# Table v of a PEER layer with 312 of 320 token columns on TensorE, the last eight tokens from gathered rows

## What is computed

```python
def block(args):
    xb, ib, gb = args                       # tokens, their 128 expert numbers, their 128 gates
    a = jax.nn.gelu(jnp.einsum('ted,td->te', u[ib], xb), approximate=False)
    return jnp.einsum('te,ted->td', gb * a, v[ib])
```

## Time and profile before

| what | us |
|---|---|
| median of 3 runs (4019.13 to 4028.27) | 4021.95 |
| the profiled execution | 4022.95 |
| its span, first to last instruction | 4021.3 |
| table v's matmuls, first to last start | 3082.2 to 3990.9 |

### The profile page before, as it was taken

The page is one execution under the profiler, slowest core; times in us unless marked ns, Lnnn a source line. Parts: engine busy times, 40 slices in busy tenths (PEclk is TensorE's granted clock), DMA queues, the critical chain, the costliest instruction groups (busy, mean ns, idle before and its releaser), DMA issues. The chain is left out here.

```text
span 4021.3 us, 70026 instructions
## 1 busy us (share of the span) xinstructions
PE 3856.3 (96%) x26200; PEld 3680.9 (92%) x26200; DVE 3056.9 (76%) x4100; ACT 1422.0 (35%) x2062; POOL 1496.8 (37%) x1285
## 2 busy tenths in 40 slices
PE   7999999999999887999999999999998999999997
PEld 7999988999999665999899999999998999999997
DVE  6875167777777433878679999999986888888887
ACT  5884122222223222223333333333333333333332
POOL 0000022323233122234215556655756555555551
PEclk9999999999999999999999999999999999999999
DMA  7988888999999797889679989888998999999996
GB/s 270 346 308 299 292 292 325 355 370 375 364 366 374 295 374 266 299 318 354 254 268 328 331 327 325 320 305 298 351 361 299 355 346 344 345 346 340 347 344 255
DMA packets 333939, 1310.11 MB, mean 326 GB/s; under 512 B 46800, under 2 KB 103280, under 8 KB 264192
## 3 DMA queue, kind: packets, MB, share of 16 engines
q1 hardware_dynamic: 201616, 646.09, 43.6%
q0 software_dynamic: 106800, 629.71, 42.5%
q10 hardware_dynamic: 25344, 31.99, 2.2%
HBM read 1237.86 MB, written 69.77 MB: 325 GB/s over the span
## 5 line engine op out<-in xcount | busy, mean ns | idle before, releaser
L130 PE MATMUL acc<-x_hi,w_hi 128*128 128x448 f32 x1296 | 478.0, 369 | 9.7 <-DVE w_lo L119 5.2
L130 PE MATMUL acc<-x_lo,w_hi 128*128 128x448 f32 x1296 | 476.3, 368 | 0.0
L114 ACT ACTIVATE w_hi<-w_raw 128x1024 fp32r<-128x1024 f32 x242 | 256.2, 1060 | 621.8 <-DMA w_raw<-in_w_gate 268.3
L130 PE MATMUL acc<-x_hi,w_lo 128*128 128x448 f32 x1296 | 476.1, 367 | 0.0
L2376 POOL DMA_INDIRECT routes_scratch<-gate_sums,route x320 | 389.0, 1216 | 139.0 <-issue 82.9
L119 DVE TENSOR_TENSOR w_lo<-w_raw,w_hi 128x1024 fp32r<-128x1024 f32 x242 | 295.6, 1223 | 185.7 <-ACT w_hi L114 184.7
L2793 POOL TENSOR_TENSOR tile_full<-act_and_gate 128x320 f32<-128x320 f32 x120 | 312.7, 2606 | 266.3 <-DVE tile_lo L2897 165.9
L2172 PE MATMUL acc<-h_hi,w_hi_b 128*128 128x320 f32 (+1 forms) x1152 | 367.4, 319 | 17.1 <-DVE w_lo_b L2162 16.9
L2154 ACT ACTIVATE w_hi_a<-w_raw 128x1024 fp32r<-128x1024 f32 x270 | 278.6, 1057 | 296.7 <-PE acc L2965 250.3
L2172 PE MATMUL acc<-h_hi,w_hi_a 128*128 128x320 f32 (+1 forms) x1152 | 367.8, 319 | 10.3 <-DVE w_lo_a L2162 9.4
L2154 ACT ACTIVATE w_hi_b<-w_raw 128x1024 fp32r<-128x1024 f32 x272 | 278.7, 1055 | 248.7 <-PE acc L2965 210.2
(11 more groups left out here) (525 smaller groups left out, 10244.5 us busy)
## 6 DMA issues: line engine op xcount, KB each, us to landing
w_raw<-in_w_peer_u SPq DMA_DIRECT2D x256, 512.0 KB, 6.5
w_raw<-in_w_peer_v SPq DMA_DIRECT2D x256, 512.0 KB, 5.8
w_first<-in_w_gate SPq DMA_DIRECT2D x96, 512.0 KB, 4.9
w_raw<-in_w_gate SPq DMA_DIRECT2D x96, 512.0 KB, 7.3
w_first<-in_w_z SPq DMA_DIRECT2D x66, 512.0 KB, 5.0
w_raw<-in_w_z SPq DMA_DIRECT2D x66, 512.0 KB, 7.2
k_ring<-in_cache_k SPq DMA_DIRECT2D x64, 512.0 KB, 6.8
v_ring<-in_cache_v POOLq DMA_DIRECT2D x64, 512.0 KB, 8.0
```

Source lines behind the costliest of these rows:

```text
L114: nc.scalar.activation(w_hi[:, j % 4, :], raw[:, j % 4, :], ACT.Copy).then_inc(q["hi"], 1)
L130: last = nc.tensor.matmul(dst, l_, r_[:, cc, 0:cn], start=(cc == first and p_ == 0), stop=(cc == last_c and p_ == 2))
```

## The change

The last eight of the 320 tokens are left out of table v's dense product, which then has NV = 312 columns. (`act_and_gate`, the tiles and `out_t` have 312 columns too.) For these eight tokens the 8 x 128 rows of v that they use are gathered: eight gathers of 128 rows, where partition p of gather k holds an expert of token p // 16. DVE multiplies each row by its weight and adds it to `sum8` (128 x 2048), in four quarters of 512 columns. At the end four matmuls with a matrix of zeros and ones (`pick`) add the 16 partitions of each token and put the sums into rows 56 to 63 of block 3, which DVE adds to x.

What this puts where:

- SP, after the load of x1's block 0: stores expert numbers, routes and gates of the eight tokens to DRAM, waits for that, and loads them in the other layout.
- POOL, after the rows of pass 1: eight gathers of single numbers (the activations), a wait for them, the weights `w8`, and the first gather of rows (`last_gather(0)`). One more `last_gather` stands ahead of the tiles of each of the stretches 1 to 7, behind a wait for the last quarter of the row before. `row8` is a single buffer.
- DVE: one quarter behind the second step of each pass of the second part of stretches 0 to 6, and of the first part of stretch 7.
- PE: the four matmuls ahead of the third pass of the last part.

```diff
-        t_hi = at("tile_hi", [P, 2 * GRP, ND], F32R, O_R1)
+        t_hi = at("tile_hi", [P, 2 * GRP, NV], F32R, O_R1)
...
+        row8 = at("rows_of_last_tokens", [P, D], F32, O_R1 + 4 * GRP * ND * 4 + 2 * D * 4)
+        sum8 = at("sum_of_last_tokens", [P, D], F32, O_R1 + 4 * GRP * ND * 4 + 3 * D * 4)
...
             sp.dma_start(x1[:, 0, :], x1_dram[COLS[0]:COLS[0] + P, :]).then_inc(s_xback, 16)
+            last8 = slice(ROWS[3] - VTOK, ROWS[3])
+            for k, x_ in enumerate((eidx, route, gate.bitcast(I32))):
+                sp.dma_start(last8_dram[k], x_[last8, 3, :]).then_inc(s_8st, 16)
+            sp.wait_ge(s_8st, 48)
+            for k, x_ in enumerate((e8, r8, g8.bitcast(I32))):
+                sp.dma_start(x_[:], last8_dram[k].rearrange("t (j k) -> (t j) k", k=VTOK)).then_inc(s_8ld, 16)
             with sp.Fori(1, (NTILE - GRP) // 2) as i:
...
+            def last_gather(k):
+                nc.gpsimd.tensor_copy(stage_8[:, 0:1], e8[:, k:k + 1] if isinstance(k, int) else e8[:, bass.ds(k, 1)]).then_inc(s_8sg, 1)
+                pool.wait_ge(s_8sg, k + 1)
+                pool.sem_inc(s_8tick, 1)
+                pool.indirect_dma_start(row8[:], None, a["peer_v"], bass.IndirectOffsetOnAxis(ap=stage_8[:, 0:1], axis=0)).then_inc(s_8gat, 16)
+
...
             for s in range(2):
                 product(s + GRP, s, 1)
-            with pool.Fori(1, (NTILE - GRP) // 2) as i:
+            rows(1, True)
+            pool.wait_ge(s_8ld, 48)
+            for k in range(VTOK):
+                pool.indirect_dma_start(a8[:, k:k + 1], None, acts_dram.rearrange("n p (t o) -> (n p t) o", o=1), bass.IndirectOffsetOnAxis(ap=r8[:, k:k + 1], axis=0)).then_inc(s_8a, 16)
+            pool.wait_ge(s_8a, 16 * VTOK)
+            nc.gpsimd.tensor_tensor(w8[:], a8[:], g8[:], ALU.mult).then_inc(s_8w, 1)
+            last_gather(0)
+            with pool.Fori(2, GRP) as i:
+                rows(i, True)
+            with pool.Fori(1, NG // 2 - 1) as gg:
+                pool.wait_ge(s_8used, 4 * gg + 1)
+                last_gather(gg)
+                with pool.Fori(0, GRP) as j:
+                    rows(GRP * gg + j, True)
+            pool.wait_ge(s_8used, 4 * (VTOK - 1) + 1)
+            last_gather(VTOK - 1)
+            with pool.Fori(GRP * (NG // 2 - 1), (NTILE - GRP) // 2) as i:
                 rows(i, True)
...
+            def row_quarter(k, j):
...
+                nc.vector.scalar_tensor_tensor(out=sum8[:, cols], in0=row8[:, cols], scalar=w, in1=sum8[:, cols],
+                                               op0=ALU.mult, op1=ALU.add).then_inc(s_8used, 1)
...
+                if s and at_row[0] is not None and par == at_row[1]:
+                    row_quarter(at_row[0], j)
...
+                if n == 2:
+                    dve.wait_ge(s_8sum, 1)
+                    dve.wait_ge(s_b3, 16)
+                    x3 = x1[0:ROWS[3], 3, :]
+                    nc.vector.tensor_tensor(x3, tps[0:ROWS[3]].rearrange("p a c -> p (a c)"), x3, ALU.add)
...
-                        last = nc.tensor.matmul(acc[:, s, h, 0:ND], l_, r_[:, t_, :], start=(c == 0 and p_ == 0),
+                        last = nc.tensor.matmul(acc[:, s, h, 0:NV], l_, r_[:, t_, :], start=(c == 0 and p_ == 0),
...
+            for j in range(GRP // 2):
+                if j == 2:
+                    pe.wait_ge(s_8used, 4 * VTOK + 1)
+                    pe.wait_ge(s_8pick, 1)
+                    pe.wait_ge(s_q0, 1)
+                    for g in range(4):
+                        last = nc.tensor.matmul(tps[0:ROWS[3], g, :], pick[:], sum8[:, 512 * g:512 * (g + 1)], start=True, stop=True)
+                    last.then_inc(s_8sum, 1)
```

More of the change, by code:

```diff
@@ L2823, in table_v_gpsimd, with sweep @@
                 rows(i, False)
-        def sweep(eng, before, split, after, beside, start=None):
+        def sweep(eng, before, split, after, beside, start, each_group):
             def body(first, par, j, build=True, ahead=True, between=None):
@@ L2914, in sums_cleared, with row_group @@
             def sums_cleared():
+                nc.vector.memset(sum8[:], 0.0)
+                nc.vector.memset(pick[:], 0.0).then_inc(s_8used, 1)
+                dve.wait_ge(s_8used, 1)
+                nc.vector.reduce_sum(pick[:, ROWS[3] - VTOK:ROWS[3]], ident[:].rearrange("p (t j) -> p t j", j=NR), AX.X).then_inc(s_8pick, 1)
                 dve.wait_ge(s_clr, 4)
                 dve.wait_ge(s_xback, 16)
+            at_row = [None, None]
+            def row_group(gg):
+                at_row[:] = [gg, 1]
+            def row_quarter(k, j):
+                known = isinstance(k, int)
+                dve.wait_ge(s_8w, 1)
+                dve.wait_ge(s_8gat, 16 * k + 16)
+                if known and k == 0:
+                    dve.wait_ge(s_8used, 1)
+                else:
+                    dve.wait_ge(s_8used, 4 * k + j - 3)
+                cols = bass.ds(512 * j, 512)
+                w = w8[:, k:k + 1] if known else w8[:, bass.ds(k, 1)]
+                nc.vector.scalar_tensor_tensor(out=sum8[:, cols], in0=row8[:, cols], scalar=w, in1=sum8[:, cols],
+                                               op0=ALU.mult, op1=ALU.add).then_inc(s_8used, 1)
             def after(i, s, par, j, build):
@@ L2943, in beside @@
                                                    op0=ALU.mult, op1=ALU.mult).then_inc(s_y0, 1)
-            sweep(dve, lambda *_: None, lambda i, s: split_lo(dve, i, s, q7), after, beside, sums_cleared)
+            sweep(dve, lambda *_: None, lambda i, s: split_lo(dve, i, s, q7), after, beside, sums_cleared, row_group)
         def table_v_tensor(pe):
@@ L2977, in table_v_tensor @@
                     half(0, 1, j, s, h)
-            with pe.Fori(1, NG // 2) as gg:
+            with pe.Fori(1, NG // 2 - 1) as gg:
                 for par in range(2):
@@ L2982, in table_v_tensor @@
                             half(gg, par, j, s, h)
+            with pe.Fori(0, GRP // 2) as j:
+                for s, h in QUARTERS:
+                    half(NG // 2 - 1, 0, j, s, h)
+            for j in range(GRP // 2):
[6 more added lines that the diff above has]
+                    last.then_inc(s_8sum, 1)
+                for s, h in QUARTERS:
+                    half(NG // 2 - 1, 1, j, s, h)
         with nc.Block() as block:
```

40 lines of the change are left out of this document (28 added, 12 removed).

## The result

The changed kernel takes **4058.89 us** (median, 4053.87 to 4075.54); the kernel before beside it 4029.64 us (4019.13 to 4037.44). The ratio is **1.0092**, 95% interval 1.0077 to 1.0107: slower by 37 us by the ratio, by 29 by the medians. Forecast were 4031 us and a range up to 4052: slower was likeliest, but the size was not in the range. The forecast started from a kernel before of 4021.95 us; beside the changed kernel it was measured 7.7 us longer, so 7.7 of the 28 us between 4031 and 4058.89 lie in the starting point and 20 in the change. The profiled execution of the changed kernel, 4053.87 us, is the fastest of its six.

What follows compares the result with a forecast made beforehand. PE's own pace was taken to bound table v. Terms -21.3 + 3.6 + 8 + 18.9 = +9.2 us on the profiled 4022.95 gave 4032, with the median 1.0 lower at 4031 us; range 4014 to 4052.

Steps and rivals of the forecast that it cites:

- PE's pace: Table v's 6144 matmuls on PE: 8 columns fewer save 3.5 ns each, taken as -21.3 us.
- 312 run as 320: Rival: 312 columns run at the pace of 320, set by weight load or issue; +30 us, chance 0.04.
- The picking matmuls: Four float32 matmuls with `pick`, 512 columns wide, alone in PE's queue near the end: +3.6 us.
- DMA 0: Table v's transfers: 8.4 MB more gathers and 1 MB fewer loads find room, costing only through later landings: 0.
- The quarters 0: DVE's 32 quarters of about 0.7 us are hidden within PE's steps: cost 0 (0 to 2).
- The start: Start of table v: SP's wait and POOL's eight small gathers delay PE up to half 12: +8 us (3 to 16).
- The heads: Heads of stretches 1 to 7: POOL's wait for DVE stalls PE, 2.2 us plus 0.5 for the clock each: +18.9 us.
- Outside the stage: Code outside table v's stage, such as nearly 30 us after its last matmul, stays as it was: 0.
- at B+1.2: Stretch head: B is when PE ends the part before; DVE's last quarter was taken as done 1.2 us later.
- After that ... the next lower part is in time: Behind a head's second stall: DVE needs 5.8 us a step, PE 6.88, so no further stall.
- the lower part at 1.2 us: Stretch head: DVE's lower part of a tile was taken to last 1.2 us.
- The delay doesn't die out: Rival: gathers landing at 8 us or later make later lower parts late, 5 to 6 us a head; 4052 us, chance 0.18.

Runs made afterwards that it cites:

- cols_mid_gather: columns_only plus the seven 1 MB gathers two passes into each stretch, without a wait and with rows nobody uses; ratio 0.9951 to the kernel before.
- heads_later: The changed kernel with POOL's gather and its wait for DVE moved later into the stretch, mostly two passes; ratio 1.0013 to the kernel before.
- before_head_waits: The kernel before (320 columns) plus POOL's wait for DVE and a small copy at each stretch's head but the first, no gather; ratio 1.0017.
- columns_only: The changed kernel without any work for the last eight tokens, their part left out of the result: 312 columns alone; ratio 0.9965 to the kernel before.

## Why the prediction was off

By its own steps, in the profiled executions (forecast +9.2, measured +30.9; the start is off by 2.3, the heads by 15.3 and what is outside by 4.2):

- **PE's pace, -21.3.** Right: 3.4 to 3.7 ns a matmul from the windows, which is 21 to 23 us, and cols_mid_gather is 20 us faster as a whole. The rival "312 run as 320" is out.
- **The picking matmuls, +3.6.** Right: 3.7.
- **DMA 0.** Right, by cols_mid_gather. **The quarters 0**: open in the middle of a stretch, wrong at the head, where the chain counts the last one and it costs 0.6 to 0.7.
- **The start, +8 (3 to 16).** Half 12 starts 9.3 us later into the stage, plus the 1.0 of gain in between: 10.3. Pass 1's weights came as forecast (PE at 3105.51, or 3101.7 counted from the stage's first start as before; forecast 3102). The eight gathers took 12.9 us instead of 10.2, since some issue in 1.2 to 2.1 us, and the lower parts again took longer beside POOL. (Between the row of pass 1 and the product of pass 2 stand eleven instructions and three waits, not ten and two.)
- **The heads, +18.9: the term that failed.** Everything from half 12 on grew by 17.4 us. With the pace's gain put back (5856 x 3.5 ns = 20.5) and 3.7 of picking taken off, 34.2 are left for the rest: 21.8 idle at the heads (forecast 15.4), 2.1 idle in the last stretch (0), and 10.3 for a slow clock and slow first matmuls (3.5). In idle time alone it is 3.1 a head against 2.2. So the 15.3 too few are 6.4 of idle time at the heads, 6.8 behind the stalls and 2.1 in the last stretch. Most of the 10.3 is the clock: over 24 us at head 1 the granted clock is 0.86 in the mean, over 20 us each at heads 5 and 7 it is 0.91, together 7.0 us of full speed lost, and 1.00 at the others.
- **Outside the stage, 0.** 4.2, in code that is the same.

Two sentences in the step on the heads were wrong. The first is that the chain starts "at B+1.2": I read it from one head of the kernel before, where POOL has its lead, and took it for all heads of a kernel that has lost it. It holds at heads 2 and 4, and there the forecast of 2.2 is met with 2.03 and 1.96, though not in its parts: 1.42 and 0.61 (0.54 at head 4) stand where 0.1 and 2.1 were forecast. The sum is met since the row's path decides when PE goes on for the second time, at B+15.9 against 16.0, and an error in the first stall only takes from the second. At the others DVE comes late. The second is "After that ... the next lower part is in time". That is right within the pass, but a lead once lost isn't won back in the stretch's eight passes, as 93 waits of ACT and 70 of DVE show. It mostly doesn't reach PE until the next head, where the chain begins at DVE: heads_later, with POOL's wait away from there, has DVE late and PE hardly stalled.

A third is smaller: the lower part at 1.2 us. I had asked what DVE's work does to POOL's product, and not what POOL's does to DVE. The pair of lower parts took 3.44 us beside a product at each of the seven heads, and 2.35 elsewhere; in before_head_waits it took 3.46 and PE had the time for it. The Trainium skill (SBUF — State Buffer, "SBUF: two separate sides") has the two engines take a shared port pair in turn, for a whole instruction; the trace agrees that one is held while the other works, here DVE by 1.1 us. Which of the two was first can't be read from it: the lower part's record begins 0.36 us before the product's (3338.20 and 3338.56), and it was the lower part that took longer.

The rival "The delay doesn't die out" has the nearest number, 4052, and its condition came true, with a median landing of 8.4 us. Its mechanism didn't: no step beyond the second came late on PE, and the second cost it 0.4 to 0.6 us, at four heads of seven. That its number lies near is luck.

## What to carry to other kernels

An engine's lead over the others is a store that covers every wait of one pass; before an edit makes it wait for the engine at the end of the chain, lay out the chain from there to the bound engine, instruction by instruction, and count from how late the first link may come, not from how it comes today. Move such a wait to where it was met long ago: two passes later, the same gathers gave PE under 1 us of stalls at the heads. And time the gain alone early: 20 us was all there was to win here.

## What the runs showed of the chip

**A gather's landing grew by 1.8 us in the median with not one byte more to move.** Its minimum, median and maximum in us, in before_head_waits, in cols_mid_gather and in the changed kernel, against the earlier trace rows:

```profile
DMA to landing us min/median/max: 5.5/8.2/13.1
```

```profile
DMA to landing us min/median/max: 5.4/8.1/11.6
```

```profile
DMA to landing us min/median/max: 5.5/8.4/11.9
```

The first of them moves the bytes of the kernel before (6.4 there), and only the moment at which POOL issues its gathers has changed; columns_only, with POOL mostly ahead, has 6.1. That the gathers now meet more of SP's loads is likely and isn't shown. The longer landing isn't what PE's stalls come from: cols_mid_gather has 8.1 and none at the heads.

**The clock.** Behind stalls of 2.26 and 5.05 us the granted clock fell to about a half, behind one of 3.26 us it stayed at 1.00. The stall's length alone doesn't tell, so a term of one size for each stall, as the forecast had it, is a mean at best: it had 3.5 us for seven heads, and 7.0 were lost at three of them.
